# Column form of the forget-gate bound, two buffers for the masked recurrence scores, depthwise filters and forget-gate sums moved up in their projections

## Chip, cores and metric

One core of one Trainium2 chip runs the whole program in one launch. The metric is the device time in microseconds (us). The kernel before took 2544.25 us (median of 3 runs, 2544.16 to 2549.97). The profiled execution took 2540.45 us by the same clock; its trace spans 2538.6 us from the first instruction to the last.

## What is computed

The reference is a stack of four transformer layers on one sequence of 256 tokens with 1024 channels, all in float32. What the change touches is in three of its mixers.

Layer 1, gated linear recurrence (8 heads of 128 channels). `q, f, i, g = h @ w_in`, four parts of 1024 columns each. The lower bound of the forget gate comes from three rows of 1024 logits:

```
lb = cumsum(softmax(lb_logits, axis=0))[0]
forget = lb + (1 - lb) * sigmoid(f);  k = 1 - forget;  q = silu(q);  v = i
out[t] = sum over s <= t of (q[t] . (k[s] * prod of forget between s and t)) v[s]
o = rms_norm(out) * norm_g * sigmoid(g);  y = o @ w_out
```

Layer 3, convolution module: `a, g = hn @ w_pw1 + b` (2048 columns), `u = a * sigmoid(g)`, a causal depthwise convolution with 31 taps over each of the 1024 channels, layer norm, silu, and a second product with 1024 columns.

Layer 4, forgetting attention (16 heads of 64 channels): keys, values and a log forget gate per head come from one product; `c` is the running sum of the log gate over the tokens; `q = hn @ w_q`; the logits are `q.k/8 + c[t] - c[s]` below the diagonal; softmax, times v, times w_o.

Between them lie a gated MLP, a differential attention (two softmaxes), a routed MLP of 8 experts, and two MLPs with squared relu.

## The kernel before, in words

**Tiling.** Tokens lie in two blocks of 128 partitions (NB = 2), channels in eight tiles of 128 (KT = 8). All large products are made of split float32: ACT rounds a weight half (128x2048) to a high part `wh` (`split`, L749 to L765), DVE subtracts it from the weights for the low part `wl` (L1288 to L1298), and PE does three products, high with high, high with low, low with high (L1912 to L1916). The activations are split in the same way (`xTh`, `xTl`). There are three buffers of halves (SPLITS = 3) and a ring of three weight chunks of 2 MB (RING = 3), filled by SP in program order; a chunk is loaded when DVE has split both halves of the chunk three before it.

**Order of the work.** Each engine has its own program, in order, and they meet at semaphores. In a projection (`project`, L1997) PE does one unit per chunk of 512 columns: half 0 for both token blocks, the turning (transposes) of the unit before (`behind`), half 1 for both blocks (`unit`, L1957). The two blocks use the two PSUM banks `up`, and a unit may begin on a bank only when DVE has worked off the result of the unit before (L1967). ACT and DVE, for each unit: split one half, apply ACT's function and DVE's step to both blocks, split the next half.

**Recurrence, projection.** The eight units take the column chunks in the order `HG_CHUNKS = [0, 1, 4, 5, 2, 3, 6, 7]` (0, 1: q; 2, 3: f; 4, 5: v; 6, 7: g). The three rows of bound logits are broadcast to all 128 partitions by a 1.5 MB transfer on POOL's queue (L633), and softmax and bound are worked out on 128x1024 tiles: DVE maxima behind unit 0 (L1370, L1371), subtractions behind unit 1 (L1374), ACT exponentials behind unit 1 (L869), sums and a reciprocal behind unit 2 (L1378 to L1380), the other reciprocal, the product and the complement behind unit 3 (L1382 to L1384). The f units need them (L1349, L1350). After the last unit the log gates are split in four pieces (ACT L880, DVE L1390).

**Recurrence, loop.** Sixteen steps n = (head, token block). For each, PE makes eight level sums (4 products of 512 columns, L2101), ACT takes their exponential (L885), DVE scales q and k with them (L1403 to L1409), PE makes the scores (L2115 to L2120), DVE masks them into one buffer `hgS` (L1418), PE multiplies them with v (L2129, L2131), ACT squares (L890) and DVE gates (L1426). For block 1 there is also a cross term: PE L2115, DVE copy L1415, PE L2129. PE's order in one turn of the loop is: level sums of n, scores of n-1, outputs of n-2. Three things tie DVE's mask to PE: the scores' banks are single, so scores of n wait for the mask of n-1 (L2111); the mask waits for the outputs of the step before, since `hgS` is single (L1417); the outputs wait for their mask (L2124).

**Convolution.** Four units of 512 columns (L2359); DVE and ACT make u, PE turns it into `uT` (two channel tiles per unit). The taps of channel tiles 0 to 3 are done on DVE (`tap`, L1717; 0.44 us per tile and tap), 12 taps of tiles 0 and 1 among the last two units (L1745 to L1748). Those of tiles 4 to 7 are done on PE as products with diagonal matrices that ACT makes (L1088 to L1093; PE L2362 to L2369), all of them after the last unit. Then PE turns the sums back (L2377).

**Forgetting attention.** After the keys and values come two units for q (L2415). The running sums of the log gate are made by PE in unit 1 (`gate_sums`: L2403 to L2413), DVE copies them (L1807), PE turns them, and ACT, after both units and all splits, copies them and writes them by two DMAs into spare rows of the keys (L1145 to L1150). Then ACT copies the second half of q (L1151), and PE starts the scores of head pair 0 when all of q has been copied (L2416 to L2418). The softmaxes follow on DVE (L1823, L1534) and ACT (L940).

Of the kernel before, what the change touches and what calls it, by code (L numbers as in the profile page):

```python
# [32 lines left out]
P = 128  # L33
D = 1024
SEQ = 256
NB = SEQ // P
KT = D // P
NH = 8
# [151 lines left out]
def _program(nc, t, ctx):  # L190
# [73 lines left out]
    hg_raw = flat(arena[:, 0:2, :])[:, 0:3 * D].rearrange("p (r n) -> p r n", r=3)  # L264
    lb, omlb = spare[:, 0:D], spare[:, D:2 * D]
# [3 lines left out]
    hgS = flat(half[:, :, :]).rearrange("p (s n) -> p s n", s=8)  # L269
# [26 lines left out]
    CV_DVE, CV_PE = range(4), range(4, KT)  # L296
# [17 lines left out]
    hg_cross = tp[:, 0, 0:P]  # L314
# [17 lines left out]
    HG_CHUNKS = [0, 1, 4, 5, 2, 3, 6, 7]  # L332
# [131 lines left out]
    hg_x = sem("hg_x")  # L464
    hg_fh, hg_fl = sem("hg_fh"), sem("hg_fl")
# [29 lines left out]
    def _(sp):  # L495
# [24 lines left out]
        for b in range(NB):  # L520
            ld(h[:, b, :], t["x"][0, b * P:(b + 1) * P, :], s_x[b])
            if b == 0:
                ld(ident, t["consts"][:, C_ID:C_ID + P], s_ident)
        for i, c in enumerate(HG_CHUNKS):
            if i == 0:
                for part, ready in enumerate((s_first, w_ready[0])):
                    ld(ring_k(c_hg)[:, 4 * part:4 * part + 4, :],
                       kp(t["hg_w_in"][part * (D // 2):(part + 1) * (D // 2), c * W:(c + 1) * W]), ready)
            else:
                cols_chunk(c_hg + i, t["hg_w_in"], c * W)  # L530
# [92 lines left out]
    def _(pool):  # L623
        nonlocal SMALL

        def small(out, in_):
# [5 lines left out]
        pool.wait_ge(s_first, 16)  # L632
        pool.dma_start(hg_raw, t["hg_lb"].rearrange("r n -> (r n)").partition_broadcast(P)  # L633
                       .rearrange("p (r n) -> p r n", r=3)).then_inc(s_lb, 16)
# [97 lines left out]
    def _(act):  # L732
# [114 lines left out]
        split(SPLITS - 1)  # L847
        for i, c in enumerate(HG_CHUNKS):
            split()
# [6 lines left out]
            for b in range(NB):  # L856
                g = g_hg + NB * i + b
                func = ACT.Sigmoid if c in (2, 3, 6, 7) else ACT.Silu if c < 2 else ACT.Copy
                step_act(g, half[:, g % 2, :], up[:, g % 2, :], func)
            if c in (2, 3):  # L860
# [4 lines left out]
            split()  # L865
            if i == 1:
                act.wait_ge(s_lbD, 1)
                for r in range(3):
                    ins = f(hg_raw[:, r, :], hg_raw[:, r, :], ACT.Exp)  # L869
                ins.then_inc(s_lbA, 1)  # L870
            elif i == 3:
# [6 lines left out]
        for x in range(2 * NB):  # L878
            at = slice((x // NB) * W, (x // NB + 1) * W)
            f(lfh[:, x % NB, at], lf[:, x % NB, at], ACT.Copy).then_inc(hg_fh, 1)  # L880
        for n in range(NH * NB + 3):
            if n < NH * NB:

                act.wait_ge(hg_m, n + 1)
                f(level_banks(n), level_banks(n), ACT.Exp).then_inc(hg_e, 1)  # L885
            if 2 <= n < NH * NB + 2:
                m = n - 2
                j, b = m // NB, m % NB
                act.wait_ge(hg_o, m + 1)
# [1624 lines left out]
```

## Time and profile before

| | |
|---|---|
| median of 3 runs | 2544.25 us |
| profiled execution | 2540.45 us (span of its trace 2538.6 us) |
| PE busy | 2383.9 us, 94% of the span, 11221 matmuls |
| PE weight loads | 1966.1 us, 77% |
| DVE busy | 1789.2 us, 70% |
| ACT busy | 1464.9 us, 58% |
| POOL busy | 56.7 us, 2% |
| mean granted TensorE clock | 0.977 of full speed |
| moved by DMA | 589.69 MB, mean 232 GB/s |

PE, DVE, ACT, POOL and SP are TensorE, VectorE, ScalarE, GpSimd and SyncE. L12 is line 12 of the kernel before. Busy time of PE is modelled, so that "busy" is not "at its peak": the start times of its instructions tell its pace. An engine's idle time is shown in square brackets with what ended it. A clock of 1.00 is 2.4 GHz, 0.50 is 1.2 GHz.

### The profile page before, as it was taken

What the parts mean: (1) busy time and instruction counts of PE and PEld (TensorE: products, weight loads), DVE (VectorE), ACT (ScalarE), POOL (GpSimd) and SP (SyncE); (2) the same over time, 40 slices, a digit from 0 to 9 for tenths busy, and PEclk for the clock granted to TensorE, in tenths of its full rate; (3) what the DMA queues carried; (4) which work ended last, traced back from release to release, by engine and by line L of the source; (5) the groups of instructions that cost most, each with busy time, mean ns of one, the idle gap of its engine ahead of it and who ended that gap; (6) DMA issues with size and microseconds to landing.
All of it is one profiled execution on the core that took longest, in us unless ns stands there. A gap on an engine that the chain in (4) does not pass through costs nothing.

```text
span 2538.6 us, 29790 instructions
## 1 busy us (share of the span) xinstructions
PE 2383.9 (94%) x11221; PEld 1966.1 (77%) x11221; DVE 1789.2 (70%) x1680; ACT 1464.9 (58%) x1562; POOL 56.7 (2%) x99
## 2 busy tenths in 40 slices
PE   7888999887999999999999999997889999889997
PEld 5677788676788888888888888886777887777886
DVE  5675554675889898989898988887765455554454
ACT  4522444363777777777777777775574446455444
POOL 0000000002200000000000000000010000000000
PEclk9999999998999999999999999998999999999999
DMA  7203554404999999999999999995403545413542
GB/s 294 104 5 117 183 193 165 172 34 153 363 333 388 326 384 331 377 337 379 335 378 336 372 342 377 340 372 198 141 4 133 199 168 180 144 68 133 197 157 78
DMA packets 264116, 589.69 MB, mean 232 GB/s; under 512 B 8417, under 2 KB 39377, under 8 KB 263760
## 3 DMA queue, kind: packets, MB, share of 16 engines
q1 hardware_dynamic: 261376, 579.38, 62.7%
q0 software_dynamic: 2608, 8.93, 1.1%
q8 instruction: 67, 1.10, 0.2%
q14 instruction: 33, 0.27, 0.0%
q10 hardware_dynamic: 32, 0.02, 0.0%
HBM read 587.22 MB, written 1.05 MB: 232 GB/s over the span
## 4 chain that ended last, share of the span: by engine, by line
PE 80%; DVE 9%; ACT 6%; DMA 3%; issue 2%; ACTq 0%; DVEq 0%; SPq 0%
PE up L1914 15%; PE up L1916 15%; PE up L1915 15%; PE acc L1914 8%; PE acc L1916 8%; PE acc L1915 8%; DVE wl L1296 4%; ACT wh L764 3%; PE up L2368 2%; DMA raw<-in_ffn_w 2%; PE acc L2235 1%; PE up L2131 1%; PE tp L2271 1%; PE acc L2117 1%; DMA raw<-in_hg_w_in 1%
## 5 line engine op out<-in xcount | busy, mean ns | idle before, releaser
L1603 DVE TENSOR_TENSOR wl<-raw,wh 128x2048 fp32r<-128x2048 f32 x378 | 864.8, 2291 | 127.2 <-ACT wh L984 124.3
L984 ACT ACTIVATE wh<-raw 128x2048 fp32r<-128x2048 f32 x378 | 727.1, 1924 | 226.9 <-PE up L1916 136.8
L1914 PE MATMUL up<-wh,xTh 128*128 128x512 f32 x1888 | 760.0, 403 | 45.3 <-DVE wl L1296 6.5
L1916 PE MATMUL up<-wh,xTl 128*128 128x512 f32 x1888 | 744.7, 394 | 0.0
L1915 PE MATMUL up<-wl,xTh 128*128 128x512 f32 x1888 | 743.9, 394 | 0.0
L1296 DVE TENSOR_TENSOR wl<-raw,wh 128x2048 fp32r<-128x2048 f32 x171 | 389.6, 2291 | 383.4 <-ACT wh L764 382.1
L764 ACT ACTIVATE wh<-raw 128x2048 fp32r<-128x2048 f32 x171 | 325.0, 1917 | 378.6 <-PE up L1916 208.7
L1914 PEld LDWEIGHTS up<-wh,xTh 128*128 128x128 f32 x1888 | 360.0, 191 | 128.0 <-issue 35.8
L1916 PEld LDWEIGHTS up<-wh,xTl 128*128 128x128 f32 x1888 | 359.3, 190 | 77.4
L1915 PEld LDWEIGHTS up<-wl,xTh 128*128 128x128 f32 x1888 | 360.6, 191 | 71.5 <-issue 0.7
L1914 PE MATMUL acc<-wh,hTh 128*128 128x512 f32 x848 | 330.7, 390 | 2.3 <-DVE hTl L1623 1.5
L1916 PE MATMUL acc<-wh,hTl 128*128 128x512 f32 x848 | 330.5, 390 | 0.0
L1915 PE MATMUL acc<-wl,hTh 128*128 128x512 f32 x848 | 330.3, 390 | 0.0
L1914 PEld LDWEIGHTS acc<-wh,hTh 128*128 128x128 f32 x848 | 159.2, 188 | 35.6 <-issue 1.7
L1916 PEld LDWEIGHTS acc<-wh,hTl 128*128 128x128 f32 x848 | 159.3, 188 | 33.0
L1915 PEld LDWEIGHTS acc<-wl,hTh 128*128 128x128 f32 x848 | 159.3, 188 | 32.8
L994 ACT ACTIVATE hTh<-tp 128x512 fp32r<-128x512 f32 x63 | 37.8, 600 | 76.5 <-PE tp L2271 76.5
L803 ACT ACTIVATE half<-up,sc 128x512 f32<-128x512 f32 x40 | 27.6, 689 | 55.0 <-PE up L1916 55.0
L2368 PE MATMUL up<-arena 128*128 128x256 f32 x248 | 55.8, 389 | 1.6 <-ACT arena L1093 1.6
L1325 DVE SCALAR_TENSOR_TENSOR xTl<-tp,vecs,xTh 128x128 fp32r<-128x128 f32 x112 | 30.3, 343 | 36.9 <-ACT xTh L784 36.6
L2368 PEld LDWEIGHTS up<-arena 128*128 128x128 f32 x248 | 48.4, 196 | 9.0 <-ACT arena L745 1.9
L1724 DVE SCALAR_TENSOR_TENSOR arena<-arena,wdw 128x256 f32<-128x256 f32 x120 | 51.2, 481 | 1.4
(360 smaller groups left out, 1950.6 us busy)
## 6 DMA issues: line engine op xcount, KB each, us to landing
raw<-in_moe_w_gate SPq DMA_DIRECT2D x126, 1024.0 KB, 6.3
raw<-in_moe_w_up SPq DMA_DIRECT2D x126, 1024.0 KB, 6.8
raw<-in_moe_w_down SPq DMA_DIRECT2D x126, 1024.0 KB, 5.8
raw<-in_ffn_w SPq DMA_DIRECT2D x32, 2048.0 KB, 8.6
raw<-in_hg_w_in SPq DMA_DIRECT2D x7, 2048.0 KB, 13.2
raw<-in_da_w_in SPq DMA_DIRECT2D x6, 2048.0 KB, 8.4
raw<-in_ffn_w_gate SPq DMA_DIRECT2D x11, 1024.0 KB, 6.9
raw<-in_ffn_w_up SPq DMA_DIRECT2D x11, 1024.0 KB, 11.0
```

The costliest lines, as they stand in the source:

```text
L764: f(wh[:, q % SPLITS, :], raw_half(q), ACT.Copy).then_inc(s_hi, 1)
L803: f(out, in_, func, **kw).then_inc(s_act, 1)
L984: f(wh[:, x % SPLITS, :], raw[:, x % RAW, :], ACT.Copy).then_inc(moe["hi"], 1)
L994: f(hTh[:, 0, :], tp[:, 0, :], ACT.Copy).then_inc(moe["Th"], 1)
L1296: V.tensor_tensor(wl[:, q % SPLITS, :], raw_half(q), wh[:, q % SPLITS, :].bitcast(F32), ALU.subtract).then_inc(s_lo, 1)
L1325: ins = V.scalar_tensor_tensor(lo[:, k, :], x[:, k, :], cols[:, gain, 4 * q + k:4 * q + k + 1], hi[:, k, :].bitcast(F32), ALU.mult, ALU.su ...
L1603: V.tensor_tensor(wl[:, x % SPLITS, :], raw[:, x % RAW, :], wh[:, x % SPLITS, :].bitcast(F32), ALU.subtract).then_inc(moe["lo"], 1)
L1724: ins = V.scalar_tensor_tensor(cT[:, k, :], src, wdw[:, k, j:j + 1], cT[:, k, :], ALU.mult, ALU.add)
L1914: mm(out, x_hi, w_hi, start=start, stop=False)
L1915: mm(out, x_hi, w_lo, start=False, stop=False)
L1916: return mm(out, x_lo, w_hi, start=False, stop=stop)
L2368: mm(up[:, k % 2, 0:SEQ], diag[:, x % DIAGS, :], uT[:, k, j:j + SEQ], start=(j == 0), stop=(j == CONV - 1)).then_inc(cv_tap, 1)
```

## The change

Recurrence, bound: the logits are loaded as 24 rows of 128 (12 KB), turned by PE into columns, and the softmax runs on 128x8 columns. The result is spread over a 128x1024 tile of diagonals, and a product with ones makes the bound as rows again, in PSUM. The waits of DVE for these steps stay behind units 0, 2 and 3; ACT's exponential moves ahead of its second split of unit 1.

Recurrence, order: the second token block of x is loaded after the first half of the first weight chunk. The chunks' order becomes 0, 1, 4, 6, 2, 3, 7, 5. The first piece of the log gates is split behind unit 6, into a buffer of its own, and level sums, exponential and scaling of step 0 are done within the last unit. Two splits of the output weights leave the last unit and stand at steps 3 and 5 of the loop. In the loop the order on PE is: scores of m, level sums of m+2, outputs of m-1; `hgS` has two buffers; the cross term has a place in the `up` bank, and ACT copies it.

Convolution: DVE's tiles are 0, 1, 2, 4, PE's 3, 5, 6, 7. Tile 3 is done before the turning of the last unit, tile 5 right after it; ACT makes diagonals among units 2 and 3. One split moves from behind unit 3 into the taps, on ACT and DVE.

Forgetting attention: the gate sums are made in q unit 0, turned in unit 1, and ACT's copy and its two DMAs stand ahead of the copies of the first half of q. The scores of heads j < 4 wait for the first half of q alone.

```diff
-    lb, omlb = spare[:, 0:D], spare[:, D:2 * D]
+    lb_rows = arena[0:3 * KT, 0, 0:P]
+    lb_cols = arena[:, 0, P:P + 4 * KT].rearrange("p (r k) -> p r k", r=4)
+    lb_diag = arena[:, 0, D:2 * D].rearrange("p (k n) -> p k n", k=KT)
+    lb, omlb = acc[:, 2:4, :].rearrange("p a n -> p (a n)"), spare[:, D:2 * D]
+    lf_first = pe_parts[:, 0, :], pe_parts[:, 1, :]
-    hgS = flat(half[:, :, :]).rearrange("p (s n) -> p s n", s=8)
+    hgS = [a.rearrange("p (s n) -> p s n", s=8) for a in (flat(half[:, :, :]), lf[:, 0, :])]
-    CV_DVE, CV_PE = range(4), range(4, KT)
+    CV_DVE, CV_PE = [0, 1, 2, 4], [3, 5, 6, 7]
-    hg_cross = tp[:, 0, 0:P]
+    hg_cross = up[:, 0, 2 * P:3 * P]
-    HG_CHUNKS = [0, 1, 4, 5, 2, 3, 6, 7]
+    HG_CHUNKS = [0, 1, 4, 6, 2, 3, 7, 5]
...
-        pool.wait_ge(s_first, 16)
-        pool.dma_start(hg_raw, t["hg_lb"].rearrange("r n -> (r n)").partition_broadcast(P)
+        pool.wait_ge(s_ident, 16)
+        pool.dma_start(lb_rows, t["hg_lb"].rearrange("r (k p) -> (r k) p", p=P)).then_inc(s_lb, 16)
...
+            if i == 6:
+                act.wait_ge(s_lbA, 2)
+                f(lf_first[0], lf[:, 0, 0:W], ACT.Copy).then_inc(hg_fh, 1)
...
             if i == 1:
                 act.wait_ge(s_lbD, 1)
-                for r in range(3):
-                    ins = f(hg_raw[:, r, :], hg_raw[:, r, :], ACT.Exp)
+                f(lb_cols[:, 0:3, :], lb_cols[:, 0:3, :], ACT.Exp).then_inc(s_lbA, 1)
...
+            if n in (3, 5):
+                split()
...
-                if m >= 1:
-                    dve.wait_ge(hg_o, m)
-                ins = V.tensor_tensor(hgS, accb[:, 1, :].rearrange("p (s n) -> p s n", s=8),
+                if m >= 2:
+                    dve.wait_ge(hg_o, m - 1)
+                ins = V.tensor_tensor(hgS[m % 2], accb[:, 1, :].rearrange("p (s n) -> p s n", s=8),
...
         dve.sem_inc(s_rows_free, 1)
-        dve.wait_ge(s_Te, T_cback)
+        dve.wait_ge(s_Te, t_cv[5] + 1)
         for j in range(CONV):
+            if j == CONV - EARLY:
+                split()
...
-        project(g_hg, t_hg, 8, T_x, 4)
-        pe.wait_ge(hg_lev, NB)
-        for n in range(NH * NB + 2):
+        project(g_hg, t_hg, 8, T_x, 4, middle=lambda c: {0: bound_turn, 3: bound_rows, 7: first_levels}.get(c))
+        pe.wait_ge(s_Te, T_hgo)
+        levels(1)
+        for m in range(NH * NB + 1):
...
+        project(g_cv, t_cv, 4, T_cv, 2, enter_cv, before_last=first_taps)
+        pe.wait_ge(s_Te, t_cv[5] + 1)
+        taps(1)
+        pe.wait_ge(s_Te, T_cback)
+        for i in range(2, len(CV_PE)):
+            taps(i)
...
-                project(d["g_q"], d["t_q"], 2, d["T_q2"], 4, middle=lambda c: gate_sums if c == 1 else None)
-                pe.wait_ge(s_Te, d["T_o"])
+                project(d["g_q"], d["t_q"], 2, d["T_q2"], 4, middle=lambda c: (gate_totals, gate_rows)[c])
...
+                    if b == 0 and j % 4 == 0:
+                        pe.wait_ge(s_Te, d["t_q"][1 if j == 0 else 3] + 1)
```

## Rows read from the trace of the kernel before

**Rows 1.** Stages: length, busy us by engine (instructions), granted clock, DMA share, GB/s

```profile
0.00:137.70 137.70, 106.81 (x457) 86.11 (x458) 84.01 (x71) 73.64 (x71) 4.29 (x10) 0.95 0.51 186
22.00:24.00 2.00, 2.00 (x11) 1.65 (x10) 0.00 (x0) 1.00 (x1) 0.00 (x0) 1.00 1.05 398
137.70:224.00 86.30, 75.75 (x585) 68.55 (x584) 57.68 (x75) 19.64 (x45) 0.00 (x0) 1.00 0.00 1
1822.80:1879.30 56.50, 55.88 (x249) 48.42 (x250) 48.76 (x113) 47.18 (x127) 0.66 (x1) 0.96 0.06 19
```

**Rows 2.** Timeline, PE in the recurrence's projection: start, us, instruction [idle before]

```profile
29.93 0.47 PE L1914 MATMUL up<-wh,xTh 128*128 128x512 f32 x1 [2.62 <-DVE stage L1356]
57.80 0.47 PE L1914 MATMUL up<-wh,xTh 128*128 128x512 f32 x1 [4.01 <-DVE arena L1358]
85.64 0.47 PE L1914 MATMUL up<-wh,xTh 128*128 128x512 f32 x1 [4.20 <-DVEq L1354]
101.19 0.47 PE L1914 MATMUL up<-wh,xTh 128*128 128x512 f32 x1 [1.93 <-DVEq L1354]
130.00 0.77 PE L2101 MATMUL acc<-hTh,xTh 128*128 128x512 f32 x1 [5.50 <-DVE xTl L1390]
```

**Rows 3.** DMA issue of the bound's logits: count, KB each, us to landing

```profile
arena<-in_hg_lb POOLq DMA_DIRECT2D x1, 1536.0 KB, 9.4
```

**Rows 4.** Timeline, two of the bound's instructions and ACT's table load in unit 4

```profile
50.24 2.96 ACT L869 ACTIVATE arena<-arena 128x1024 f32<-128x1024 f32 x3 [4.46 <-DVE arena L1374]
63.49 3.35 DVE L1380 RECIPROCAL raw<-raw 128x512 f32<-128x512 f32 x1
...
78.03 1.28 ACT L803 ACT_TABLE_LOAD   x1
```

**Rows 5.** Timeline, first mask of the loop, then two steps of PE's loop

```profile
137.73 1.22 DVE L1418 TENSOR_TENSOR half<-acc,big 128x1024 f32<-128x1024 f32 x1
...
188.34 1.80 PE L2117 MATMUL acc<-raw 128*128 128x128 f32 x14 [0.48 <-DVE half L1418]
...
192.91 0.39 PE L2101 MATMUL acc<-hTh,xTl 128*128 128x512 f32 x1
...
199.29 1.80 PE L2117 MATMUL acc<-raw 128*128 128x128 f32 x14 [0.48 <-DVE half L1418]
```

**Rows 6.** Groups by line and shape, 137.7 to 225 us: count, busy us, mean ns, idle before

```profile
L1418 DVE TENSOR_TENSOR half<-acc,big 128x1024 f32<-128x1024 f32 x16 | 19.6, 1224 | 16.6 <-PE up L2131 16.6
L1403 DVE TENSOR_TENSOR raw<-acc,arena 128x1024 f32<-128x1024 f32 x7 | 8.6, 1225 | 3.6 <-ACT acc L885 3.6
L885 ACT ACTIVATE acc<-acc 128x1024 f32<-128x1024 f32 x7 | 7.1, 1008 | 7.2 <-PE acc L2101 7.2
```

**Rows 7.** Timeline of the convolution: ACT in unit 2, PE's last product, turning, DVE's last taps

```profile
1803.44 0.42 ACT L1077 ACTIVATE half<-half 128x256 f32<-128x256 f32 x1 [2.54 <-DVEq L1738]
...
1815.73 0.39 PE L1916 MATMUL up<-wh,xTl 128*128 128x512 f32 x1
1818.92 0.44 PE L1948 MATMUL tp<-cst,stage 128*128 128x128 f32 x2 [2.80 <-DVE stage L1742]
1868.67 4.29 DVE L1724 SCALAR_TENSOR_TENSOR arena<-arena,wdw 128x256 f32<-128x256 f32 x10
1879.25 1.07 PE L2377 MATMUL tp<-cst,arena 128*128 128x128 f32 x8 [0.61 <-issue]
```

**Rows 8.** Groups by line and shape, 1822.8 to 1879 us

```profile
L2368 PE MATMUL up<-arena 128*128 128x256 f32 x248 | 55.8, 389 | 1.6 <-ACT arena L1093 1.6
L1296 DVE TENSOR_TENSOR wl<-raw,wh 128x2048 fp32r<-128x2048 f32 x1 | 2.3, 2293 | 1.4 <-ACT wh L764 1.4
```

**Rows 9.** Timeline between the q projection and the softmaxes of layer 4

```profile
2227.53 0.60 ACT L796 ACTIVATE raw<-tp 64x512 f32<-64x512 f32 x1
...
2232.82 1.91 ACT L764 ACTIVATE wh<-raw 128x2048 fp32r<-128x2048 f32 x1 [3.47 <-PE up L1916]
...
2235.16 1.25 ACTq L1150 DMA_DIRECT2D arena<-ncT  x1
...
2239.58 0.80 PE L2423 MATMUL up<-arena 128*128 128x128 f32 x2 [5.36 <-ACT raw L796]
2241.94 0.40 ACT L940 ACTIVATE arena<-arena,att 128x128 f32<-128x128 f32 x1 [1.11 <-DVE att L1534]
```

More of the change, by code:

```diff
@@ L847, in _, with decays @@
         split(SPLITS - 1)
+        def decays(n):
+            act.wait_ge(hg_m, n + 1)
+            f(level_banks(n), level_banks(n), ACT.Exp).then_inc(hg_e, 1)
         for i, c in enumerate(HG_CHUNKS):
-            split()
+            if i < 7:
+                split()
             if i > 0 and HG_CHUNKS[i - 1] < 4:
@@ L1069, in _, with conv_sum, diagonals @@
         row_roots(H_CV)
+        def conv_sum(i):
+            k = CV_PE[i]
+            act.wait_ge(cv_tap, CONV * (i + 1))
+            f(cT[:, k, :], acc[:, i, 0:SEQ], ACT.Identity, bias=rowcols[:, 0, k:k + 1]).then_inc(cv_sum, 1)
+        def diagonals(xs):
+            for x in xs:
+                if x >= DIAGS:
+                    act.wait_ge(cv_tap, x - DIAGS + 1)
+                if x % CONV == DIAGS and x > CONV:
+                    conv_sum(x // CONV - 1)
+                f(diag[:, x % DIAGS, :], ident, ACT.Copy, scale=wdw[:, CV_PE[x // CONV], x % CONV:x % CONV + 1]).then_inc(cv_diag, 1)
         for c in range(4):
@@ L1141, in _ @@
                     if c == 1:
+                        act.wait_ge(f_CT, 1)
+                        f(ncT[0:NH2, :], acc[0:NH2, 1, 0:SEQ], ACT.Copy, scale=-1.0).then_inc(f_ct, 1)
+                        act.wait_ge(f_ct, 1)
+                        act.wait_ge(s_Te, d["t_kv"][3] + 1)
+                        for z in range(2):
+                            act.dma_start(kz[z][BIAS_ROWS[z], :, :], ncT[z:NH2:2, :]).then_inc(s_kb, 16)
                         for b in range(NB):
@@ L1336, in _, with scaled @@
         split(SPLITS - 1)
+        def scaled(n):
+            j, b = n // NB, n % NB
+            dve.wait_ge(hg_e, n + 1)
+            if n == 0:
+                dve.wait_ge(s_Te, T_hgo)
+            if n >= 2:
+                dve.wait_ge(hg_s, n - 1)
+            if n >= 3 and b == 1:
+                dve.wait_ge(hg_o, n - 2)
+            ev = level_banks(n).rearrange("p a w -> p (a w)").rearrange("p (s n) -> p s n", s=8)
+            at = slice(b * P, (b + 1) * P)
+            over = lambda x, levels: x[:, j, at].unsqueeze(1).broadcast_to([P, levels, P])
+            V.tensor_tensor(hgA[:, n % 2], ev, over(qT, 8), ALU.mult)
+            if b == 0:
+                V.tensor_tensor(hg_far[:, j % 2, :], ev[:, 0, :], kT[:, j, at], ALU.mult)
+                ins = V.tensor_tensor(hgB[:, n % 2, 1:8], ev[:, 1:8], over(kT, 7), ALU.mult)
+            else:
+                ins = V.tensor_tensor(hgB[:, n % 2], ev, over(kT, 8), ALU.mult)
+            ins.then_inc(hg_ab, 1)
         for i, c in enumerate(HG_CHUNKS):
-            split()
+            if i < 7:
+                split()
             for b in range(NB):
+                if i == 7 and b == 1:
+                    scaled(0)
                 s = NB * i + b
@@ L1388, in _ @@
+        for x in range(1, 2 * NB):
             at = slice((x // NB) * W, (x // NB + 1) * W)
@@ L1743, in _ @@
             if b == NB - 1:
-                split()
+                if c < 3:
+                    split()
                 if c >= 2:
@@ L2357, in enter_cv, with taps @@
                 turn_ready(T_cv, H_CV, BLOCK[b])
[L2359 to L2364 removed]
+        def taps(i):
+            k = CV_PE[i]
             for j in range(CONV):
```

199 lines of the change are left out of this document (97 added, 102 removed).

## The prediction

> **What bounds the kernel now.** I read the stages first, then PE's timeline in each stage that the diff touches. PE is busy for 94% of the span and its clock is at 1.00 nearly everywhere, so only time in which PE idles, or runs at 1.2 GHz, can be taken back: PE's products themselves hardly change. The stages [rows 1] say where that time lies. Up to 137.7 us PE is busy for 106.8 us, so 31 us are idle. In the recurrence's loop 75.75 of 86.3 us are busy, so 10.6 us are idle. During the taps PE is busy throughout. PE's timeline then names the waits of the projection [rows 2]: 2.62 us before unit 1, 4.01 before unit 3, 4.20 before unit 5, 1.93 before unit 6, 5.50 before the first level sums. In the loop [rows 5] PE waits about 0.5 us for DVE's mask in every step. Before the taps it waits first for DVE, then for ACT's first diagonal [rows 7]. Before layer 4's softmaxes it waits 5.36 us for ACT's copies of q [rows 9]. The rest of the program is not touched and should only shift.
>
> The sum is made against the profiled execution's own 2540.45 us (1.85 us more than its span). It is 3.8 us under the median of the three runs, 2544.25 us; the forecast lies between what the two would give.
>
> **1. Start and the 12 KB load.** The broadcast of the logits, 1.57 MB, leaves the queues [rows 3]. At the 398 GB/s that the engines move then [rows 1] it holds them for 4.0 us, all of it before the second weight chunk has landed. x's second block (0.52 MB) now comes behind the first half chunk, so PE begins 1.3 us earlier by the same rate. Unit 1 waits 2.62 us because DVE splits two halves of that chunk before it serves unit 0's results. I take unit 1 as beginning at 27.0 instead of 29.93 us: **-2.9**. Bounds: -1.3 (only the reordering counts) and -4.0 (all of the transfer).
>
> **2. Bound chain before unit 3.** ACT's first split in unit 2 stands behind a wait of 4.46 us for DVE's subtractions and three exponentials of 2.96 us [rows 4]; DVE's share of that split stands ahead of its copy of unit 2's result, for which unit 3 waits. The subtractions and exponentials become four DVE operations on 24 or 8 columns and one exponential with its table load, together some 2.5 us by my estimate, beside unit 2's 11 us of products. ACT's split can then begin when unit 2's first half is done, 5 us before that unit's end, and split and copy (1.9, 2.3, 0.4 us) are over 0.5 us before unit 3. So the 4.01 us go, and what they cause: unit 3 begins at half clock, its first ten products are 0.43 us apart where the others are 0.23, 1.7 us in all. Next late is that same copy, with 0.5 us to spare. PE gains two small jobs in units 0 and 3, the turn and a float32 product with ones on two banks: 1.0 us from the level sums' four products of 0.23 us [rows 5]. Together **-4.7** (-5.7 +1.0). Bounds: -5.7, and 0 if the chain now waits for its own semaphores.
>
> **3. Before unit 5.** DVE's second reciprocal (another 3.35 us like the one shown [rows 4]), a product and a complement delay the split and, behind it, the f unit's four operations. Now only the complement is left, read from PSUM. Unit 5 must still wait for DVE's four operations on block 0, as unit 6 does for 1.93 us [rows 2]; 1.28 us of that is a table load [rows 4] that unit 4 no longer has, since the g unit ahead of it uses the same function. I take 1.0 us: 3.2 less, and 1.7 of half clock less: **-4.9**. Bounds: -2.3 (the wait stays at 1.93 and the clock low) and -5.9.
>
> **4. End of the projection to the first mask.** Now: last product at 124.5, first mask at 137.73 [rows 5], 13.2 us, with the 5.50 us wait [rows 2]: ACT's split, four copies, two of DVE's subtractions, level sums at half clock, exponential with table load, two scalings. After: step 0's level sums (+0.9 on PE) and exponential lie inside the last unit; behind it come DVE's scaling of step 0 (2.4 us), one copy, one subtraction, level sums of step 1 (1.7, half clock after 3 us idle), exponential 1.0, scaling 2.4. Chained from the last product I get 8.6 us for the mask: **-3.7** (-4.6 +0.9). Bounds: 0 and -6.
>
> **5. The loop.** One step takes 5.48 us: 10.95 us from 188.34 to 199.29 for two [rows 5]. It is a ring: mask 1.22 [rows 6], scores 1.8, outputs 1.8, and the hand-overs; the level sums fill the time of the mask. With two mask buffers the mask of m no longer waits for the outputs of m-1, and PE runs level sums of m+2 and outputs of m-1 (2.7 us) while DVE masks (1.22 and some 0.2 of hand-over). PE's own work becomes the bound: scores 1.79, outputs 1.71 to 1.80, level sums 0.95, cross terms 0.45 in two steps, 4.77 us a step. The scaling of m+2 (exponential 1.0, then 2.3 [rows 6]) has almost two steps' time. DVE has 57.7 us of work in the loop [rows 1], less eight copies that go to ACT (2.2), plus two splits of 2.29 [rows 8]: 60 of 75 us, so each split may cost PE about 1.3 us, once. First mask to last output: the old 86.2 us become 14 steps of 4.77 us less one set of level sums, the first handover, the last mask and outputs and 2.6 for the splits, 75.0: **-11.2**. Bounds: -13 (splits free) and 0 (below).
>
> **6. Taps.** PE's last product is at 1815.9, the last 124 taps run 1822.81 to 1878.6 (248 passes, 55.8 us [rows 8], of which 2 us are lost at half clock), and the turning back begins at 1879.25 [rows 7]. Tile 3 needs only what unit 1 made, so PE goes on at 1816.1: 53.8 us at full clock and 0.9 of turning end at 1870.8. DVE ends its taps at 1872.96 [rows 7], its 1.4 us wait for ACT's split [rows 8] goes, its work is the same: 1871.6. So DVE becomes the last to end, by 0.8 us, and the turning begins at 1871.9: **-7.3**. Hidden: ACT's 16 early diagonals, eight in unit 2 and eight in unit 3, at an estimated 0.3 us each, fit its wait of 2.54 us in unit 2 [rows 7] and the longer one in unit 3; were they late, unit 3 would slip by some 2 us. The moved split stands on DVE's path either way. Bounds: -5 and -8.
>
> **7. Bias rows.** ACT's copy and two DMA issues (the first 1.25 us, some 2.3 in all) move ahead of the first half's copies, where ACT idles 3.47 us before its last split [rows 9]. After the projection ACT has the split, four copies of 0.6 us and the table load, and the scores of head pair 0 do not wait for these copies. PE's wait for DVE's copy of the sums, just under 1 us, goes too. First exponential at 2237.5 instead of 2241.94 [rows 9]: **-4.5**. The DMAs are small and have 4 us to land. Queued behind the new ACT wait for the turned sums is the first half of q, which nobody needs for 5 us. Bounds: -2.5 (a late landing) and -6.
>
> **Sum.** -2.9 -4.7 -4.9 -3.7 -11.2 -7.3 -4.5 = -39.2. From 2540.45 that is 2501.3, from the median 2505.1. **Forecast 2503 us.**
>
> **Rival A, DVE binds the loop** (chance 0.16). DVE is in order: a step's mask stands behind the scaling of the next. Where that scaling waits for level sums (0.95), exponential (1.0), itself (2.35), and then the mask (1.22) must come before PE goes on, the ring is 5.5 us again, as now. Against: level sums are issued a step and a half ahead. For: for odd steps the scaling also waits for the cross term of three steps before. It gives 2503 + 11 = 2514.
>
> **Rival B, the projection finds other waits** (chance 0.15). Terms 1 to 4 are 16.2 us and rest on orders in which each engine is just in time; if transfers hold unit 1 and DVE's new waits stand behind units 0, 2 and 3, half is left: 2511. With A, 2522.
>
> **Rival C, the clock** (chance 0.02), the other side. In the loop the granted clock is 1.00 with 0.5 us idle in each step [rows 1, 5]. If the new order, which uses every PSUM bank in turn, made it fall to 1.2 GHz, PE's 75.75 us would take 151, and the time would be 2503 + 76 = 2579. It decides against the change once more than 41 us of PE's full-rate work runs at half clock. Against: the level fell only where PE had idled 3 us and more, and the new order idles less.
> The Trainium skill (TensorE: Matmul & The Clock Gate, A second HAM failure mode: psum-queue depth-cycling) says that short idles between groups of matmuls that cycle through the banks make the clock go back and forth. By that rule the loop would already be slow; the trace of before disagrees, with 1.00 over the loop [rows 1].
>
> **Rival D, moved splits only** (chance 0.02): within 0.3% of before, which would need A, B and lost terms 6 and 7 together. 0.3%, some 8 us, is about what a measurement of this kernel can tell from no change.
>
> **How the numbers follow.** The forecast has 0.65. The low end takes terms 1 to 7 nearer to their good bounds (another 9 us), 2494; the high end takes in A and B together, 2522. Faster 0.96, same 0.02, slower 0.02.
>
> **What would show it.** Right: no PE wait above 1.5 us before units 3 and 5; first mask near 121 us; loop steps of 4.8 us with PE at 97% busy and no wait of the mask for PE's outputs; taps end near 1871 less the shift of 27 us, with DVE last; first exponential of layer 4 some 39 us earlier. Wrong: DVE busy above 90% in the loop, steps above 5.2 us, a clock under 0.95 there, or a wait before unit 1 for the second chunk as long as now. I would be wrong on the total if an untouched stage moved by more than its shift.

## The result, and the profile of the changed kernel

The changed kernel takes 2508.5 us (median of 4 executions, 2505.41 to 2509.39). The kernel before takes 2546.93 us beside it (4 executions, 2544.16 to 2549.97). The ratio is 0.9847, with a 95% interval of 0.9834 to 0.9861, so the change saves 38 us; the forecast was 2503 us, and the time lies in its range. A second comparison on one chip (5 executions against 9) gives 2508.17 and 2548.81 us, ratio 0.9842 [0.9826, 0.9858].

The profiled execution of the changed kernel took 2509.39 us, with a span of 2507.5. Its page shows PE busy for a larger share of a shorter span, 95% (before 94%), and the taps' 248 passes:

```profile
span 2507.5 us, 29792 instructions
PE 2376.7 (95%) x11226; PEld 1964.7 (78%) x11226; DVE 1773.5 (71%) x1671; ACT 1459.2 (58%) x1568; POOL 56.8 (2%) x99
...
L2427 PE MATMUL acc<-arena 128*128 128x256 f32 x248 | 53.9, 378 | 0.0
```

The passes take 53.9 us instead of 55.8 [rows 8]. The stages, which answer to [rows 1] (projection up to the first mask, loop, convolution):

```profile
core 0: us, PE busy (x) PEld busy (x) DVE busy (x) ACT busy (x) POOL busy (x), PEclk, DMA share, GB/s
0.00:123.00 123.00, 104.97 (x465) 84.75 (x465) 66.75 (x68) 68.45 (x68) 4.34 (x10) 0.99 0.55 195
123.00:201.00 78.00, 73.66 (x581) 70.84 (x582) 59.28 (x69) 24.00 (x54) 0.00 (x0) 0.98 0.01 1
...
1763.00:1849.00 86.00, 84.11 (x391) 71.32 (x390) 72.79 (x142) 58.08 (x148) 0.65 (x1) 1.00 0.22 80
```

Up to the first mask PE now idles for 18 us (before 31), in the loop for 4.3 (before 10.6). PE's timeline holds the waits that are left in the projection and the loop; it answers to [rows 2, 5]:

```profile
27.09 0.47 PE L1956 MATMUL up<-wh,xTh 128*128 128x512 f32 x1 [1.39 <-DVE stage L1407]
...
75.88 0.47 PE L1956 MATMUL up<-wh,xTh 128*128 128x512 f32 x1 [1.45 <-DVEq L1405]
...
89.85 0.47 PE L1956 MATMUL up<-wh,xTh 128*128 128x512 f32 x1 [1.92 <-DVEq L1405]
...
118.54 0.47 PE L2152 MATMUL tp<-hTl,xTh 128*128 128x512 f32 x1 [2.86 <-DVE xTl L1445]
...
124.40 3.33 PE L2174 MATMUL acc<-raw 128*128 128x128 f32 x14 [2.00 <-DVE half L1457]
...
136.95 1.80 PE L2174 MATMUL acc<-raw 128*128 128x128 f32 x14 [1.24 <-DVE half L1457]
...
147.87 1.80 PE L2174 MATMUL acc<-raw 128*128 128x128 f32 x14 [1.24 <-DVE half L1457]
```

There is no wait before unit 3 any more; that before unit 5 fell from 4.20 to 1.45 us, and the one ahead of the level sums behind the projection from 5.50 (then step 0's) to 2.86 (now step 1's). In the loop PE waits three times for a mask. Behind the third, PE has no wait above 0.5 us until the end of the loop, and two steps take 9.44 us (before 10.95). The third and the second of these waits come from DVE's moved splits, of which this is the first:

```profile
133.39 2.28 DVE L1322 TENSOR_TENSOR wl<-raw,wh 128x2048 fp32r<-128x2048 f32 x1
135.59 1.22 DVE L1457 TENSOR_TENSOR half<-acc,big 128x1024 f32<-128x1024 f32 x1
```

The end of the taps (all engines) answers to [rows 7], ACT's queue ahead of layer 4's softmaxes to [rows 9]:

```profile
1843.63 4.69 DVE L1763 SCALAR_TENSOR_TENSOR arena<-arena,wdw 128x256 f32<-128x256 f32 x11
1843.76 3.19 PE L2427 MATMUL acc<-arena 128*128 128x256 f32 x14
...
1848.43 1.09 PE L2448 MATMUL tp<-cst,arena 128*128 128x128 f32 x8 [1.48 <-DVEq L1795]
...
2197.72 0.36 ACT L1169 ACTIVATE ncT<-acc 16x256 f32<-16x256 f32 x1
2198.11 1.26 ACTq L1173 DMA_DIRECT2D arena<-ncT  x1
...
2206.88 1.28 ACT L957 ACT_TABLE_LOAD   x1
2208.18 0.40 ACT L957 ACTIVATE arena<-arena,att 128x128 f32<-128x128 f32 x1
```

DVE is the last to end its taps. The bias rows stand ahead of ACT's last split (2202.51); the first exponential comes 33.8 us earlier, 4.8 more than the 28.9 by which everything had shifted at the end of layer 3's expert stage. From these landmarks of the two traces, and of a second trace of each kernel (taken with the experiments below), the stages last, in us. The convolution's first turn is the first transpose of a finished unit there, the turning back the transpose of the finished taps:

| stage | before | before, 2nd | changed | changed, 2nd |
|---|---|---|---|---|
| start to first mask | 137.73 | 138.52 | 123.04 | 121.46 |
| first mask to last output | 86.2 | 86.2 | 78.1 | 76.5 |
| to the convolution's first turn (not touched) | 1562.4 | 1562.3 | 1562.1 | 1563.6 |
| to the turning back | 92.9 | 92.9 | 85.3 | 85.3 |
| to layer 3's first expert turn | 58.1 | 58.1 | 56.9 | 56.8 |
| layer 3's expert stage (not touched) | 162.8 | 163.8 | 165.9 | 165.9 |
| to layer 4's first expert turn | 219.6 | 219.1 | 215.2 | 215.2 |
| layer 4's expert stage (not touched) | 164.1 | 165.7 | 166.3 | 165.7 |
| to the end (not touched) | 54.8 | 54.8 | 54.8 | 54.8 |
| span | 2538.6 | 2541.3 | 2507.5 | 2505.3 |

So in the first pair of traces the start, the loop, the convolution and the stretch ahead of layer 4's expert stage give back 34.8 us, the other rows take 3.7 of it, and the spans differ by 31.1.

### The profile page after: what moved, and what is told of

Same layout as the page of the kernel before. It is cut to its first block, busy times and chain, and to the rows that moved or that the text cites. A ratio compares the mean times of both kernels' runs of the same rounds, so it can differ in the third digit from the quotient of the medians.

```text
span 2507.5 us, 29792 instructions
## 1 busy us (share of the span) xinstructions
PE 2376.7 (95%) x11226; PEld 1964.7 (78%) x11226; DVE 1773.5 (71%) x1671; ACT 1459.2 (58%) x1568; POOL 56.8 (2%) x99
## 4 chain that ended last, share of the span: by engine, by line
PE 75%; DVE 11%; ACT 7%; DMA 5%; issue 2%; ACTq 0%; DVEq 0%; SPq 0%
PE up L1956 15%; PE up L1958 15%; PE up L1957 15%; PE acc L1956 7%; PE acc L1958 7%; PE acc L1957 7%; DVE wl L1322 5%; DMA raw<-in_ffn_w 4%; ACT wh L769 4%; DVE arena L1763 2%; PE acc L2297 1%; PE tp L2333 1%; PE up L2193 1%; PE acc L2174 1%; PE tp L1937 1%
## 5 line engine op out<-in xcount | busy, mean ns | idle before, releaser
L1011 ACT ACTIVATE hTh<-tp 128x512 fp32r<-128x512 f32 x63 | 37.8, 601 | 76.5 <-PE tp L2333 76.5
L1937 PE MATMUL tp<-cst,h 128*128 128x128 f32 x176 | 28.6, 309 | 27.1 <-DVEq L1301 7.8
L2427 PE MATMUL acc<-arena 128*128 128x256 f32 x248 | 53.9, 378 | 0.0
```

The lines of the kernel that those rows point to most:

```text
L1011: f(hTh[:, 0, :], tp[:, 0, :], ACT.Copy).then_inc(moe["Th"], 1)
L1937: ins = nc.tensor.transpose(tp[:, tt % 2, k * P:(k + 1) * P], src[:, b, (4 * q + k) * P:(4 * q + k + 1) * P], ident)
L2427: mm(acc[:, i, 0:SEQ], diag[:, x % DIAGS, :], uT[:, k, j:j + SEQ], start=(j == 0), stop=(j == CONV - 1)).then_inc(cv_tap, 1)
```

## The experiments

Each kernel ran once or five times, and a single time has no interval: these experiments rest on stage lengths in the traces. The kernel before took 2548.41 us (one run) beside the two runs on mask buffers, the splits behind the mask and the transfer back, 2548.25 us (one run) beside the kernel before once more, late taps, late bias rows and freed banks, and 2548.81 us (median of 9) beside the others.

**The kernel before, with two mask buffers and nothing else.**

```diff
-    hgS = flat(half[:, :, :]).rearrange("p (s n) -> p s n", s=8)
+    hgS = [a.rearrange("p (s n) -> p s n", s=8) for a in (flat(half[:, :, :]), lf[:, 0, :])]
...
-                if m >= 1:
-                    dve.wait_ge(hg_o, m)
+                if m >= 2:
+                    dve.wait_ge(hg_o, m - 1)
```

> The kernel before with two buffers of masked scores and nothing else; the order of the loop on PE stays as before. Theory (the ring mask, scores, outputs was the bound, and PE's own work is next): the loop, from the first mask to the last output product, falls from 86.2 us to 77 to 80 us, the step from 5.48 to 4.75 to 4.95 us, the whole kernel is 6 to 9 us faster than before. Rival A (DVE, in order, binds the loop as soon as the ring is gone): step 5.3 us or more, less than 3 us gained.

Measured: 2544.81 us, only 3.6 less than before where 6 to 9 were expected, but the loop did what the theory said. First mask to last output takes 77.2 us instead of 86.2. Two steps take 9.95 us on DVE:

```profile
160.38 1.22 DVE L1418 TENSOR_TENSOR half<-acc,big 128x1024 f32<-128x1024 f32 x1
...
170.33 1.22 DVE L1418 TENSOR_TENSOR half<-acc,big 128x1024 f32<-128x1024 f32 x1
```

So the buffer alone brings 9.0 us. They did not reach the end because this execution ran more at half clock ahead of the loop (first mask at 140.44 instead of 137.7 to 138.5 us) and because the stretch between the expert stages (222.6 us beside 219.1 to 219.6) and layer 4's expert stage (168.9 beside 164.1 to 165.7), which the edit doesn't touch, were longer. Why they were longer in this one execution is not shown.

**The changed kernel, with one mask buffer.**

```diff
-                if m >= 2:
-                    dve.wait_ge(hg_o, m - 1)
-                ins = V.tensor_tensor(hgS[m % 2], accb[:, 1, :].rearrange("p (s n) -> p s n", s=8),
+                if m >= 1:
+                    dve.wait_ge(hg_o, m)
+                ins = V.tensor_tensor(hgS[0], accb[:, 1, :].rearrange("p (s n) -> p s n", s=8),
```

> The changed kernel with one buffer of masked scores, so that each mask waits again for the outputs of the step before; the new order on PE stays. Theory: the new order alone is worse than the old one, since level sums and outputs now lie between the scores and their mask: scores 1.8, level sums 0.95, outputs 1.9, mask and hand-over 1.5, a step of 6.1 us, the loop about 98 us instead of 78.1, the kernel 18 to 22 us slower than the changed one. Rival: the order is what brings the gain, the step stays under 5.5 us and the kernel within 10 us of the changed one.

Measured: 2531.99 us, 23 more than the changed kernel; first mask to last output takes 99.9 us, 21.8 more than in the first trace of the changed kernel, 23.4 more than in the second. The mask's line (what it waited for, then who waited for it):

```profile
L1457 DVE TENSOR_TENSOR half<-acc,big x16: 1215/1224/1225, 122.4 to 217.4; 128x1024 f32<-128x1024 f32 x16
its engine sat idle before it (us, times) until:
  PE up L2193: 37.3, 15
who waited for it (us, times):
  PE acc L2174: 21.8, 15
```

Steps take 6.43 us, more than the old 5.48, and the loop's 99.9 us are 13.7 more than the 86.2 of the old order with one buffer: with one buffer the new order, outputs behind the next level sums, is the worse one. The order is only right together with the second buffer.

**The moved splits of the loop, on DVE placed behind the mask.**

```diff
-            if n in (3, 5):
-                split()
             if 1 <= n <= NH * NB:
                 m = n - 1
...
                 ins.then_inc(hg_sm, 1)
+            if n in (3, 5):
+                split()
```

> The changed kernel with DVE's splits of steps 3 and 5 behind the mask of that turn of the loop, not ahead of it. Theory (each of these splits holds up a mask, and PE waits 1.24 us for it twice): both waits of 1.24 us go, the loop takes 75.5 to 76.5 us instead of 78.1, the kernel gains about 2 us. Rival: DVE has no room for the 2.29 us in any place near, and the wait only moves to the next step: 78 us.

Measured: 2504.51 us; first mask to last output takes 73.9 us. Both waits of 1.24 us are gone, and the only one of the loop above 0.5 us is the first. DVE's timeline shows the split behind the mask, at no cost to the next one:

```profile
131.06 1.22 DVE L1455 TENSOR_TENSOR half<-acc,big 128x1024 f32<-128x1024 f32 x1
132.19 2.28 DVE L1322 TENSOR_TENSOR wl<-raw,wh 128x2048 fp32r<-128x2048 f32 x1
...
136.91 1.22 DVE L1455 TENSOR_TENSOR arena<-acc,big 128x1024 f32<-128x1024 f32 x1
```

Against the second trace of the changed kernel (76.5 us, no half clock in the loop) that is 2.6 us, what the forecast had charged for the two splits.

**The large transfer put back.** The broadcast of the logits (1.57 MB) is loaded again, to a place where nothing reads it, and DVE waits for it behind unit 0.

```diff
+        pool.wait_ge(s_first, 16)
+        pool.dma_start(flat(arena[:, 3:5, :])[:, 0:3 * D].rearrange("p (r n) -> p r n", r=3),
+                       t["hg_lb"].rearrange("r n -> (r n)").partition_broadcast(P)
...
+                dve.wait_ge(s_back, 16)
```

> The changed kernel plus the 1.5 MB broadcast of the bound's logits, loaded into memory that is free then and not used; DVE waits for it behind unit 0. It prices the transfer alone. Theory: the second weight chunk lands 3 to 4 us later, unit 1 begins at 29.5 to 30.5 us instead of 27.09, and the first mask comes 2 to 3 us later. Rival (the weights were not held up by it, the gain of unit 1 came from the order of x): unit 1 begins before 28 us.

**x's two blocks loaded ahead of the first weights, as before; the short load stays.**

```diff
         ld(ident, t["consts"][:, C_ID:C_ID + P], s_ident)
+        ld(h[:, 1, :], t["x"][0, P:2 * P, :], s_x[1])
...
-                    if part == 0:
-                        ld(h[:, 1, :], t["x"][0, P:2 * P, :], s_x[1])
```

> The changed kernel, with both blocks of x loaded ahead of the first weights, as before; the short load of the logits stays. Theory (the start's gain is the 1.57 MB transfer that left the queues, not x's order): unit 1 begins within 0.4 us of the changed kernel's 27.1 us. Rival (the reordering brought 1.3 us of it, as the bound of the prediction had it): unit 1 begins 1 to 1.5 us later, at 28.1 to 28.6 us.

Measured: 2513.67 and 2515.3 us. With the transfer back: PE's first products of units 0 and 1, and between them ACT's first split of the second weight chunk. Then, with the old order of x, PE's first product of unit 0 and the same split:

```profile
13.80 0.79 PE L1963 MATMUL up<-wh,xTh 128*128 128x512 f32 x1 [0.95 <-DVE wl L1328]
...
23.30 3.73 ACT L775 ACTIVATE wh<-raw 128x2048 fp32r<-128x2048 f32 x2 [7.80 <-DMA raw<-in_hg_w_in]
...
30.23 0.47 PE L1963 MATMUL up<-wh,xTh 128*128 128x512 f32 x1 [3.28 <-DVE stage L1413]
```

```profile
15.97 0.80 PE L1955 MATMUL up<-wh,xTh 128*128 128x512 f32 x1 [6.00 <-DVE wl L1321]
...
20.43 1.92 ACT L768 ACTIVATE wh<-raw 128x2048 fp32r<-128x2048 f32 x1 [3.47 <-DMA raw<-in_hg_w_in]
```

With the transfer back unit 0 still begins early (13.80; 13.28 in the changed kernel, 14.59 before), but unit 1 comes 3.1 us later than in the changed kernel: it is held by the second chunk, which ACT begins at 23.30 (20.16 in the changed kernel, 23.00 before). So the order of x alone gives nothing. The first mask comes at 128.65 us, 5.6 to 7.2 us later, where 2 to 3 were expected: behind the wait of 3.28 us unit 1 takes 13.6 us instead of 12.0, and unit 6 is as long, as in the first trace of the changed kernel.

With the old order the second chunk is early (20.43), unit 0 begins 2.7 us later, and unit 1 follows it without a wait, at 29.60 us instead of 27.09. My expectation that x's order was worth nothing fell, and the rival's 1 to 1.5 us was too small as well. Unit 1 begins at the later of two times, the end of unit 0 and DVE's service behind the second chunk, so that the gains of the two halves don't simply add up. What the short load alone is worth stays open: in this one run unit 0 began 1.0 to 1.4 us later than in the traces of the old program, which has the same order of x, for a reason that I did not find. Had it begun at 14.6 to 15.0 us and lasted 12.7 to 13.4 us, as in the traces of the old program, unit 1 would begin at 27.3 to 28.4 us by this estimate.

**The kernel before once more.**

> The kernel before, unchanged, in one more execution. In the profiled executions layer 3's and layer 4's expert stages took 162.8 and 164.1 us before and 165.9 and 166.3 us after, though the change doesn't touch them. Theory (this execution of before was a fast one, and its stages vary by themselves): here they take 165 to 166.5 us each, the stretch between them 219.6, and the whole 2544 to 2548 us. Rival (the change makes them longer, through what it leaves in other places in memory): here again 162.5 to 164.5 us each.

Measured: 2543.16 us; the expert stages take 163.8 and 165.7 us, the stretch between them 219.1. That is between the two theories, and the expectation's 2544 us was missed too. In all eleven traces of the changed kernel and its variants layer 3's stage took 165.6 to 166.3 us and layer 4's 165.1 to 167.2; in three runs with the old program (one with two mask buffers) 162.8, 163.8 and 164.3, and 164.1, 165.7 and 168.9. For layer 3 the two groups don't overlap; for layer 4 they do.

**All four of PE's tap columns behind the last turning.** ACT's diagonals from the 17th on move there too.

```diff
-        project(g_cv, t_cv, 4, T_cv, 2, enter_cv, before_last=first_taps)
-        pe.wait_ge(s_Te, t_cv[5] + 1)
-        taps(1)
+        project(g_cv, t_cv, 4, T_cv, 2, enter_cv)
         pe.wait_ge(s_Te, T_cback)
-        for i in range(2, len(CV_PE)):
+        for i in range(len(CV_PE)):
```

> The changed kernel, but all four of PE's convolution columns begin behind the last turning, as before; DVE's taps still start early and the moved split stays. Theory (PE's early column is what the stretch gained): PE starts its 124 taps some 4 to 7 us behind its last product, is the last to end again, and the turning back comes 6 to 7 us later than in the changed kernel: 2514 to 2516 us beside 2509. Rival (DVE's earlier start and the split did it, and PE would have been done in time): at most 1.5 us later, DVE still last.

Measured: 2519.35 us. PE's timeline, first taps and the turning back:

```profile
1800.69 1.65 PE L2426 MATMUL acc<-arena 128*128 128x256 f32 x3 [0.47 <-ACT arena L750]
...
1857.77 1.07 PE L2445 MATMUL tp<-cst,arena 128*128 128x128 f32 x8 [0.61 <-issue]
```

From unit 2's turn (1788.98 here, 1786.87 in the changed kernel) to the turning back it is 68.8 us instead of 61.6: 7.2 us, and PE no longer waits for DVE there. PE's early columns are what this stage gained. The whole is 11 us longer, as the untouched middle, too, was longer in this execution: 1566.8 us (1562.1 to 1564.6 in all others).

**Layer 4's bias rows behind ACT's last split.**

```diff
                     if c == 1:
-                        act.wait_ge(f_CT, 1)
...
                     split()
+                act.wait_ge(f_CT, 1)
```

> The changed kernel, but ACT makes layer 4's bias rows (copy and two transfers) behind its last split, as before. Theory (their place in ACT's queue was worth most of the term): the first exponential of that attention comes 2.5 to 4.5 us later than in the changed kernel, 2512 to 2514 us in all. Rival (the gain came from PE's sums made earlier and from scores that no longer wait for all of q): at most 1.5 us later.

Measured: 2510.85 us. ACT's timeline:

```profile
2205.03 0.37 ACT L1172 ACTIVATE ncT<-acc 16x256 f32<-16x256 f32 x1
2205.43 1.25 ACTq L1176 DMA_DIRECT2D arena<-ncT  x1
...
2209.82 1.28 ACT L957 ACT_TABLE_LOAD   x1
```

From the end of layer 3's expert stage to this table load it is 139.6 us instead of 135.7, and to layer 4's expert stage 218.7 instead of 215.2. So ACT's order is 3.5 of the 3.9 to 4.3 us that the stretch ahead of this stage gained. The total shows only 2 us of it; 2512 to 2514 us had been expected.

**PE's bank freed by ACT's copy instead of by DVE's use of the copy**, in the first projection.

```diff
+                if g >= 2:
+                    act.wait_ge(s_st, g - 1)
...
-                        pe.wait_ge(s_st, g - 1)
+                        pe.wait_ge(s_act if g < g_hg + 8 * NB else s_st, g - 1)
```

> The changed kernel, but in the first projection PE writes a PSUM bank again as soon as ACT has copied it out, instead of when DVE has used the copy; ACT waits for DVE before it writes that copy again. Theory (what is left of the waits before units 1, 5 and 6, 1.39, 1.45 and 1.92 us, is this order alone): they are gone or under 0.5 us, the first mask comes 4 to 6 us earlier, with what half clock followed them, and the whole is 2503 to 2506 us. Rival (DVE's splits are late as well and hold PE next): under 2 us gained.

Measured: 2502.24 us. The waits of 1.39, 1.45 and 1.92 us are gone, and the next wait of PE is that for step 1's parts, 2.92 us before 111.63; the first mask comes at 117.12 us, 4.3 to 5.9 us earlier. From 24 to 110 us PE is busy for 84.7 of 86 us (in the changed kernel 85.1 of 90 from 24 to 114):

```profile
24.00:110.00 86.00, 84.70 (x385) 68.90 (x383) 52.50 (x56) 54.33 (x56) 2.86 (x4) 1.00 0.52 186
```

**The better versions.** First the two edits together (splits behind the mask, banks freed by ACT), then with a third, the split of step 1's log gates made ahead of the last copies:

```diff
                 if i == 7 and b == 0:
                     decays(0)
+                    f(lfh[:, 1, 0:W], lf[:, 1, 0:W], ACT.Copy).then_inc(hg_fh, 1)
...
             V.tensor_tensor(hgA[:, n % 2], ev, over(qT, 8), ALU.mult)
+            if n == 0:
+                dve.wait_ge(hg_fh, 2)
+                V.tensor_tensor(lfl[:, 1, 0:W], lf[:, 1, 0:W], lfh[:, 1, 0:W].bitcast(F32), ALU.subtract).then_inc(hg_fl, 1)
```

> The changed kernel with two edits of single runs together: DVE's two moved splits behind the mask (2504.5 us alone) and PE's banks freed by ACT's copy (2502.2 us alone). The two act on different stretches, the loop and the projection. Theory (they add): first mask at 116 to 118 us, 73.5 to 74.5 us from it to the last output, 2498 to 2500 us. Rival (the loop's gain in the single run was mostly a difference between executions): loop 76 us or more, 2502 or more.

> The same two edits, and step 1's high and low part of the log gates made before ACT's and DVE's last copies: ACT converts it as soon as the last product is done, DVE subtracts it between two operations of the scaling of step 0. Theory (PE's wait of 2.9 us before step 1's level sums is the order on ACT and DVE): the wait is 1.3 to 1.7 us, the first mask comes 1 to 1.5 us earlier than in the run with the two edits, 2497 to 2498.5 us. Rival (the scaling of step 0 is now late by as much as it was moved back): first mask within 0.3 us.

> The changed kernel once more, beside the other two on this chip: 2506 to 2510 us, and a second trace of it. If half clock falls at places that differ between executions, the stretches at 1.2 GHz (89.9 to 93.7 us and 124.4 to 127.7 us in the first trace) lie elsewhere here or are missing; if it follows from the instructions alone, they lie in the same places.

| kernel, 5 executions each | median | lowest, highest | ratio to before, 95% interval | first mask | mask to last output |
|---|---|---|---|---|---|
| changed | 2508.17 | 2506.06, 2510.27 | 0.9842 [0.9826, 0.9858] | 121.46 | 76.5 |
| two edits | 2504.02 | 2495.68, 2508.14 | 0.9824 [0.9802, 0.9847] | 116.52 | 73.9 |
| three edits | 2499.70 | 2498.39, 2505.47 | 0.9813 [0.9795, 0.9830] | 115.41 | 75.5 |

In the traces the two edits add up: the last output comes 7.5 us earlier than in the changed kernel's trace of that chip, and the span is 2496.9 against 2505.3 us. The timing is less clear. The mean of five is 5.3 us lower, with executions 12 us apart, so the times alone don't separate the two kernels; the median was not in the 2498 to 2500 us expected, nor is that of the three edits in its 2497 to 2498.5. With the third edit the mean is 7.5 us lower than the changed kernel's, beyond the scatter (an interval of about 3.4 us either way). But the third edit itself brought nothing in the trace: the wait of 2.92 us fell to 1.60 and the first mask came 1.1 us earlier, and PE paid part of it back at the next mask.

```profile
110.64 0.47 PE L2160 MATMUL tp<-hTl,xTh 128*128 128x512 f32 x1 [1.60 <-DVE xTl L1382]
...
116.77 2.04 PE L2182 MATMUL acc<-raw 128*128 128x128 f32 x14 [2.04 <-DVE half L1463]
```

That wait was 1.11 us with two edits. The last output comes at 190.92 us with three edits and 190.41 with two, in a trace in which unit 0 had begun 1.3 us later, and the turning back at 1838.9 and 1839.0 us. Both versions can be used in place of the changed kernel.

## Why the prediction was right, term by term

The sum was -39.2 us from a profiled execution of 2540.45. The traces give -31 there, and -36 between the second pair; the medians give -38.4 and -40.6. The profiled executions of the kernel before were fast ones: 2540.45 us is less than all nine of the last comparison (2540.97 to 2552.14), 2543.16 less than eight of them. Where the others spent their extra time no trace shows. So that the medians come as near to -39.2 as they do is in part luck: the traces show 3 to 8 us less.

- **Term 1, start (-2.9): right, -2.84.** Its lower bound was not: I had priced "only the reordering counts" at -1.3, and the run with the transfer back has unit 1 at 30.23 us, no earlier than before. What the short load gives alone stays open.
- **Term 2, before unit 3 (-4.7): right, -4.2.** The end of unit 4 moved from 81.44 to 74.43, 7.0 with term 1. The wait and its half clock went. The float32 product with ones was dearer than estimated: its four instructions are 1.88 us in PE's timeline, where I had taken about 0.9 from the level sums.
- **Term 3, before unit 5 (-4.9): -4.3.** The wait is 1.45 us where I took 1.0. The run with the other semaphore shows that this rest was no bound of DVE, as I had called it ("unit 5 must still wait for DVE's four operations"): PE waited for DVE's use of a copy where only ACT's eviction was needed.
- **Term 4, to the first mask (-3.7): right in direction, more was there.** The chain from the last product to the first mask takes 7.4 us, where I had summed 8.6. That is -5.0 in the first trace, from which half clock in unit 6 must be kept apart: that unit's end moved by 9.7 us only, 1.6 less than unit 5's. Terms 1 to 4 were -16.2; the two pairs of traces give -14.7 and -17.1.
- **Term 5, the loop (-11.2): the mechanism right, the size off.** -8.1 in the first trace, -9.8 in the second pair. The steady step is 4.72 us where I had 4.77, and the splits cost 2.6 where I had 2.6. What failed was the two ends. The steps and the splits are as summed: 68.4 us from the second to the last scores in the second trace, and 14 times 4.77, less 0.95, plus 2.6. For "the first handover, the last mask and outputs" the sum left 6.6 us, and they take 8.1: 1.4 from the first mask to the scores behind it (of the 2.00 us in which PE has nothing to do), and 6.7 from the start of the last scores to the last output, with a wait of 0.46 us. The first trace adds 1.6 us: its scores behind the wait of 2.00 us ran at half clock, 3.33 us instead of 1.80. Of the gain, the second buffer alone is 9.0 us; with PE's new order, the cross terms copied by ACT and the splits placed well it is 12.3. No run separates the new order from ACT's copies.
- **Term 6, taps (-7.3): right, -7.6,** with DVE the last to end by 1.48 us (forecast 0.8). The run with late taps gives 7.2 of it back.
- **Term 7, bias rows (-4.5): right, -4.3 and -3.9,** 3.5 of it from ACT's order.
- **What the sum left out:** the untouched stages, which I had said "should only shift". Layer 3's expert stage became 3.1 and 2.1 us longer, the stretch ahead of it 1.2 shorter (last section). That was a sign I had named for being wrong on the total, and the time lies in the range all the same. Two other signs did not come: PE is busy for 94% of the loop, not 97%, and layer 4's first exponential comes 33.8 us earlier, not 39.

**The rivals.** A (DVE binds the loop, 2514) fell: DVE is busy for 59 of 78 us there, and a mask holds PE only at the start and behind a split. B (the projection finds other waits, 2511) fell: at most 1.5 us of terms 1 to 4 is missing in one trace, nothing in the other. C (the clock in the loop, 2579) fell: after the first scores the granted clock is at full speed, 2.4 GHz, through the whole new order; the loop's mean is 0.98 in the first trace, and 1.00 in the second, from the first mask at 121.46 to the last output at 197.91 us. The rule of the Trainium skill (TensorE: Matmul & The Clock Gate, A second HAM failure mode: psum-queue depth-cycling) would have had the loop go back and forth; here too the traces disagree: the level falls once in the loop of the first (0.57 from 124 to 128 us) and not at all in that of the second. D (moved splits only) fell with the total.

## What to carry to other kernels

An order of work and a buffer belong together: with one mask buffer the changed loop is 13.7 us longer than the old one (99.9 against 86.2), with two and the splits behind the masks it is 3.3 us shorter (73.9 against 77.2), so neither is to be judged alone. A filler such as a weight split cost nothing here right behind the instruction that another engine waits for, and 1.3 us each ahead of it. And of every wait for an engine that is merely last in a row, ask which step really frees the resource: PE's waits in the first projection were for a reader of a copy, not of its bank, and went with two changed waits.

## What the runs showed of the hardware

**Half clock comes and goes between executions of the same instructions.** The granted clock by 4 us windows, changed kernel, first trace and second trace:

```profile
88.00:92.00 4.00, 2.15 (x6) 1.74 (x7) 3.51 (x7) 2.48 (x3) 0.00 (x0) 0.78 1.02 389
92.00:96.00 4.00, 4.00 (x15) 3.22 (x15) 1.44 (x2) 2.44 (x2) 0.00 (x0) 0.79 0.29 107
124.00:128.00 4.00, 3.60 (x17) 3.63 (x18) 2.58 (x4) 0.00 (x0) 0.00 (x0) 0.57 0.02 4
```

```profile
88.00:92.00 4.00, 2.18 (x10) 1.82 (x11) 3.51 (x7) 2.45 (x3) 0.00 (x0) 1.00 1.04 393
92.00:96.00 4.00, 4.00 (x22) 3.36 (x21) 1.43 (x2) 2.80 (x3) 0.00 (x0) 1.00 0.27 101
124.00:128.00 4.00, 4.00 (x34) 3.83 (x33) 2.21 (x4) 2.19 (x2) 0.00 (x0) 1.00 0.01 4
```

In both, PE idled 1.9 us at 88, 2.9 us ahead of step 1's level sums and 2.0 us for the first mask. In the first trace the clock fell to 1.2 GHz behind the first and the last of these, for some 3.4 us each; in the second it did not fall at all from 20 to 144 us. Four more runs with the same instructions up to there fell only between 116 and 124 us. In the old program, with idle times of 4.0, 4.2 and 5.5 us, it fell behind all three, in all three traces. I had said that the level fell only where PE had idled 3 us and more; here it fell in one trace of six behind the wait of 1.9 us. The trace of the kernel before shows that my sentence was wrong for it as well: at 1768.46 us PE goes on after 2.04 us of idle, and the granted clock is 0.61 from 1768 to 1772 us.

**Half clock moved into a stage that the change doesn't touch.** Layer 3's expert stage begins with the same idle time of 1.96 us in every trace. Its first 8 us before, in the first trace of the changed kernel, and in the second:

```profile
1936.00:1940.00 4.00, 2.68 (x15) 2.18 (x16) 4.00 (x4) 3.08 (x4) 0.00 (x0) 1.00 0.00 0
1940.00:1944.00 4.00, 4.00 (x20) 3.29 (x19) 1.41 (x3) 0.00 (x0) 0.00 (x0) 1.00 0.00 0
```

```profile
1904.00:1908.00 4.00, 2.72 (x12) 2.20 (x13) 4.00 (x4) 3.04 (x4) 0.00 (x0) 0.77 0.00 0
1908.00:1912.00 4.00, 4.00 (x16) 3.26 (x15) 1.37 (x3) 0.00 (x0) 0.00 (x0) 0.81 0.00 0
```

```profile
1904.00:1908.00 4.00, 4.00 (x15) 3.13 (x14) 3.71 (x4) 1.39 (x3) 0.00 (x0) 0.57 0.00 0
1908.00:1912.00 4.00, 4.00 (x19) 3.32 (x18) 0.00 (x0) 0.00 (x0) 0.00 (x0) 1.00 0.00 0
```

At 0.77 and 0.81, and at 0.57, 1.7 us of full-speed time are missing in each, which is most of the 2.1 to 3.1 us that this stage grew. The stretch ahead of it got 1.2 us shorter; behind the norm there the half clock lasts less long than before (in 4 us windows 0.50, 0.50, 0.92 before, 0.54, 0.60, 1.00 in the changed kernel). Together the two became 0.9 us longer in the second pair of traces and 1.9 in the first. It is so in all traces: behind the norm the granted clock is at 1.2 GHz for 10.2 us in the three of the old program, and at 2.4 GHz at the stage's start; in the eleven of the changed kernel and its variants it is 6.8 us behind the norm and 3.4 us at the stage's start. What decides where the clock falls stays open: no run here was made for it.
